# Moving the places at which the split weight buffers begin in SBUF

## The chip, the cores and the metric

The kernel runs on one core of one Trainium2 chip. Its time is the device time of one execution in microseconds (us).

## What is computed

Two transformer-like blocks over 256 tokens of width 2048, one after the other, all in float32. Cut to the products with large weights, which are nearly all of the work:

```python
# first block
h = rmsnorm(x, g[0]);  proj = h @ w_in                     # 2048 -> 6736
y_pool, y_conv, y_attn = mixers(proj)                      # small work beside
up    = einsum('bsnc,ncd->bsnd', [y_pool, y_conv, y_attn], w_branch)
gates = sigmoid(h @ w_gate + b_gate)                       # 2048 -> 3 * 2048
x = x + rmsnorm((sum(gates * up)) @ w_out, g[1])
x = x + rmsnorm(square(relu(rmsnorm(x, g[2]) @ w_up)) @ w_down, g[3])   # 2048 -> 8192 -> 2048
# second block
h = modulate(rmsnorm(x), silu(c) @ w_ada + b_ada);  p = h @ w_in_2
y = (g_a * ((attn * silu(z_a)) @ w_pa) + g_b * ((fourier(u_b) * silu(z_b)) @ w_pb)) @ w_o
out = rmsnorm(x + gate * y)
```

## The kernel before, in words

Every large product is a job, and every job is cut into chunks of KC = 2 blocks of 128 weight rows by 512 weight columns (512 KB, 4 KB in each partition). There are 768 chunks, numbered q, and each engine takes them in that order. A chunk passes through four hands:

1. SyncE loads it from HBM into one of five `raw` buffers.
2. ScalarE copies it into a high buffer `whi` in the format float32r (`high`, line 906).
3. VectorE subtracts the high part from the raw one and writes the rest into a low buffer `wlo` (`low`, line 1234). It works AHEAD = 3 chunks ahead of TensorE.
4. TensorE multiplies (`chunk`). The other operand, the activations, is split in the same way, into pairs such as `op0h` and `op0l`. Each product is three matmuls: high by high, high by low, low by high.

High and low buffers number NSPL = 4 each, and chunk q uses number q % 4. ScalarE may write a high buffer again when TensorE has finished the chunk four back.

A job has one of two modes. In mode T (280 chunks) the activations are the stationary operand, 128 columns, and the split weights are the moving one, 512 columns: 12 matmuls a chunk, lines 867, 868 and 869. In mode W (488 chunks) it is the other way round: the weights are stationary, 128 columns, and the activations move, 256 columns: 24 matmuls a chunk (18 in one job with 384 weight columns), lines 874, 875 and 876. Every matmul loads stationary weights of its own. One job, `vw`, is a mode T job with 272 moving columns in place of 512. Long runs of jobs in one mode follow each other; the order is that of `job_list`. Between chunks stand short side parts (transposes, attention scores, sums over partitions), for which TensorE leaves the chain of chunks for a moment.

Addresses in a partition: `line(shift)` moves the next free place to `shift` bytes past a multiple of 256. All operand buffers (`op0h`, `op1h`, `yah`, `hch`, `mgh` and their low halves) begin 64 bytes past a multiple of 256. In a split buffer, mode T chunks begin at 64 past it and mode W chunks at 128 past it. Inside a buffer the pieces that one matmul reads are 512, 1024 or 2048 bytes apart, so the place past a multiple of 256 is the same for all of them.

Of the kernel before, what the change touches and what calls it, by code (L numbers as in the profile page):

```python
# [10 lines left out]
ACT = mybir.ActivationFunctionType  # L11
AX = mybir.AxisListType.X
F32 = mybir.dt.float32
F32R = mybir.dt.float32r
# [3 lines left out]
KC = 2  # L18
NRAW = 5
NSPL = 4  # L20
# [118 lines left out]
def program(nc, a, out, scratch_e, scratch_x):  # L139
    ctx = ExitStack()  # L140
    with ctx:
# [51 lines left out]
        for u in range(12):  # L193
            q = of["vw"].end + 1 + 2 * u
# [6 lines left out]
        for g in range(4):  # L201
            q = (of["pool0"].end + 1, of["pool0"].end + 5, of["pool1"].end + 1, of["pool1"].end + 5)[g]
# [5 lines left out]
        for i in range(4):  # L208
            q = of["pool1"].end + 11 + 2 * i
# [5 lines left out]
        for i in range(4):  # L215
            q = of["q1"].end + 2 + 10 * i
# [10 lines left out]
        for j in range(12):  # L227
            q = ada_at[8 * j + 7]
# [3 lines left out]
        for tt in range(2):  # L232
            q = of["b23"].end + tt
# [3 lines left out]
            q = of["wo3"].end + 1 + tt  # L237
# [3 lines left out]
            q = of["dn33"].end + 1 + tt  # L241
            side(dve_at, q, "mlp_add", tt)
            q = of["dn33"].end + 2 + tt
# [3 lines left out]
        for s, q0 in ((1, of["wo0"].first + 6), (2, of["kc"].first + 5), (3, of["vc"].first + 7)):  # L247
            for i in range(8):
                q = q0 + i // 2
# [3 lines left out]
        for s, name in enumerate(("kc", "k", "qq0", "qq1", "qq2")):  # L253
            q = of[name].end
# [7 lines left out]
        for i in range(6):  # L262
            q = heads2[i]
# [10 lines left out]
        for g in range(4):  # L274
            q = of["zb"].end + 4 * g
# [8 lines left out]
        top = [(nc.sbuf_base + 63) // 64 * 64]  # L284

        def at(name, shape, off, dt=F32):
            return nc.alloc_sbuf_tensor_at(name, shape, dt, offset=off)

        def sb(name, shape, dt=F32):
            size = 4 * int(np.prod(shape[1:]))  # L290
            t = at(name, shape, top[0], dt)
            top[0] += (size + 31) // 32 * 32
            return t

        raw = [sb(f"raw{i}", [128, KC, 512]) for i in range(NRAW)]
        def line(shift):

            top[0] += (shift - top[0]) % 256
            return top[0]

        def split_buffers(name):

            w = {"T": [], "W": []}
            for i in range(NSPL):
                o = line(64)
                for mode, shift in (("T", 0), ("W", 64)):
                    w[mode].append(at(f"{name}{mode}{i}", [128, KC, 512], o + shift, F32R))
                top[0] = o + 64 + 4 * KC * 512
            return w

        whi, wlo = split_buffers("whi"), split_buffers("wlo")
        op0_at = line(64)
        op0h, op0l = sb("op0h", [128, 16, 256], F32R), sb("op0l", [128, 16, 256], F32R)
# [88 lines left out]
        def pair_of(job):  # L402
            return bank[2 * job.pair], bank[2 * job.pair + 1]
# [6 lines left out]
        def sem(name):  # L410
            return ctx.enter_context(nc.semaphore("s_" + name))

        s_raw = [sem(f"raw{i}") for i in range(NRAW)]
        s_hi, s_lo, s_pe = sem("chunk_high"), sem("chunk_low"), sem("chunk_done")
# [105 lines left out]
        landed, fills = {}, [0] * NRAW  # L520
# [91 lines left out]
        def _(pe):  # L612
# [217 lines left out]
            def operand_wait(job, k):  # L830

                if job.x in ("x0", "ctx", "x1", "x2"):
                    pe.wait_ge(s_oper, 8 * ("x0", "ctx", "x1", "x2").index(job.x) + k // 2 + 1)
                elif job.x == "pool":
                    pe.wait_ge(s_plo, k // 2 + 1)
                elif job.x == "conv":
                    pe.wait_ge(s_clo, k // 2 + 1)
                elif job.x == "ya":
                    pe.wait_ge(s_ya, k + 2)
                elif job.x == "mix":  # L840
                    pe.wait_ge(s_mix, k // 2 + 1)
                elif job.x == "att":
                    pe.wait_ge(s_att, k + 2)
                elif job.x == "four":
                    pe.wait_ge(s_four, k + 2)
                elif job.x == "mg":
                    pe.wait_ge(s_mg, k // 2 + 1)
                else:
                    pe.wait_ge(s_hid, 8 * job.arg[0] + k // 2 + 1)

            def chunk(q, tts=(0, 1)):
                job, k = chunks[q]
                banks = pair_of(job)
                xh, xl = hi_of[job.x], lo_of[job.x]
                h, l = whi[job.mode][q % NSPL], wlo[job.mode][q % NSPL]
                if k == 0 and job.before:
                    pe.wait_ge(s_pair[job.pair], job.before)
                if job.fresh:
                    operand_wait(job, k)
                pe.wait_ge(s_lo, q + 1)  # L860
                for kk in range(KC):
                    ka, first, last = job.kt0 + k + kk, k + kk == 0, k + kk == job.nkt - 1
                    if job.mode == "T":
                        for tt in tts:
                            o = banks[tt][:, 0:job.n]
                            th, tl = xh[:, ka, 128 * tt:128 * tt + 128], xl[:, ka, 128 * tt:128 * tt + 128]
                            pe.matmul(o, th, h[:, kk, 0:job.n], start=first, stop=False, skip_group_check=True)  # L867
                            pe.matmul(o, th, l[:, kk, 0:job.n], start=False, stop=False, skip_group_check=True)  # L868
                            mm = pe.matmul(o, tl, h[:, kk, 0:job.n], start=False, stop=last, skip_group_check=True)  # L869
                    else:  # L870
                        for m in range(job.n // 128):
                            o = banks[m // 2][:, 256 * (m % 2):256 * (m % 2) + 256]
                            wh, wl = h[:, kk, 128 * m:128 * m + 128], l[:, kk, 128 * m:128 * m + 128]
                            pe.matmul(o, wh, xh[:, ka, :], start=first and m % 2 == 0, stop=False, skip_group_check=True)  # L874
                            pe.matmul(o, wh, xl[:, ka, :], start=False, stop=False, skip_group_check=True)  # L875
                            mm = pe.matmul(o, wl, xh[:, ka, :], start=False, stop=last, skip_group_check=True)  # L876
                if 1 in tts:
                    mm.then_inc(s_pe, 1)
                elif q == NQ - 1:
                    mm.then_inc(s_o2first, 1)  # L880
# [7 lines left out]
            for q in range(NQ - NSPL):  # L888
                for name, arg in pe_at[q]:
                    parts[name](*arg)  # L890
                chunk(q)
            for tt in range(2):
                for q in range(NQ - NSPL, NQ):
                    chunk(q, (tt,))
# [4 lines left out]
        def _(act):  # L899
            def high(q):  # L900
                job, k = chunks[q]
                i, v = landed["w", q]
                act.wait_ge(s_raw[i], v)
                if q >= NSPL:
                    act.wait_ge(s_pe, q - NSPL + 1)
                act.activation(whi[job.mode][q % NSPL][:, :, 0:job.n], raw[i][:, :, 0:job.n], ACT.Copy).then_inc(s_hi, 1)  # L906

            def square(src, junk, name, tt):
                act.activation(junk, src[:, tt, :], ACT.Square, accum_out=norm_col(name, tt)[0]).then_inc(s_sumsq, 1)
# [301 lines left out]
            for i in range(3):  # L1211
                turn_x(i)
                high(i)
            for q in range(NQ):
                for name, arg in act_at[q]:
                    parts[name](*arg)
                if q + AHEAD < NQ:
                    high(q + AHEAD)
                if q in ends and ends[q].ep in eps:
                    if q < NQ - 1:  # L1220
                        act.wait_ge(s_pe, q + 1)
                    eps[ends[q].ep](ends[q], *pair_of(ends[q]))
# [4 lines left out]
        def _(v):  # L1227
            own = Steps(s_dve)

            def low(q):  # L1230
                job = chunks[q][0]
                x, h = raw[landed["w", q][0]][:, :, 0:job.n], whi[job.mode][q % NSPL][:, :, 0:job.n]
                v.wait_ge(s_hi, q + 1)
                v.tensor_tensor(wlo[job.mode][q % NSPL][:, :, 0:job.n], x, h.bitcast(F32), ALU.subtract).then_inc(s_lo, 1)  # L1234

            summed = [0, 0]

# [449 lines left out]
            for i in range(4):  # L1687
                x = x0[:, 1, 512 * i:512 * i + 512]
# [4 lines left out]
            for i in range(3):  # L1693
                turn_x(i)
                low(i)
            for q in range(NQ):
                for name, arg in dve_at[q]:
                    parts[name](*arg)
                if q + AHEAD < NQ:
                    low(q + AHEAD)  # L1700
                    for i in ada_after[q + AHEAD]:
                        ada(i)
                if q == NQ - 1:
                    ep_o2_last(ends[q], *pair_of(ends[q]))
                elif q in ends and ends[q].ep in eps:
                    v.wait_ge(s_pe, q + 1)
                    eps[ends[q].ep](ends[q], *pair_of(ends[q]))
# [24 lines left out]
```

## Time and profile before

| | us |
|---|---|
| median of 2 runs | 2303.47 (2302.29 to 2304.64) |
| the profiled execution | 2306.96 |
| its span, first to last instruction | 2305.1 |
| TensorE busy (matmuls) | 2274.0 (99%) |
| VectorE busy | 1468.4 (64%) |
| ScalarE busy | 1070.8 (46%) |
| mean granted TensorE clock | 0.996 of 2.4 GHz |

Matmuls are pipelined and their recorded durations overlap, so what counts for TensorE is not the duration of one but the step from the start of one to the start of the next. A window of the trace that holds nothing but matmuls gives it: its length by their number (two or three of those counted lie across its edges). The execution has 1.9 us outside its span.

### The profile page before, as it was taken

How to read it: one execution, taken by the hardware profiler on the slowest of the kernel's cores; microseconds unless marked ns; L12 is line 12 of the kernel's file. 1: busy time of each engine (PE TensorE's matmuls, PEld its weight loads, DVE VectorE, ACT ScalarE, POOL GpSimd, SP SyncE). 2: the span in 40 equal slices, each digit the busy share in tenths (PEclk: the TensorE clock that was granted, in tenths of full speed). 3: DMA queues.
4: the chain of work that ended last, by engine and by line, in shares of the span. 5: the costliest groups of instructions: out<-in, count | busy, mean ns of one | idle time of the engine just before them, and what ended most of it. 6: DMA issues, size and time to landing. Idle time of an engine off the chain costs nothing.

```text
span 2305.1 us, 37604 instructions
## 1 busy us (share of the span) xinstructions
PE 2274.0 (99%) x15980; PEld 2116.1 (92%) x15980; DVE 1468.4 (64%) x1844; ACT 1070.8 (46%) x1422; POOL 40.4 (2%) x61
## 2 busy tenths in 40 slices
PE   7999999999999999999999999999999999999998
PEld 7889999999999988988988988998889979999987
DVE  6757578787887667544555555555756545577665
ACT  5444435444344456544443443444656545434443
POOL 1000000000000001000000000000100000000000
PEclk9999999999999999999999999999999999999999
DMA  8855676677777765666656656656664444778763
GB/s 273 253 158 163 192 218 222 219 229 240 247 230 251 250 226 176 186 202 192 186 192 192 186 189 197 195 181 209 230 203 132 145 118 139 248 273 274 252 214 138
DMA packets 246368, 473.73 MB, mean 206 GB/s; under 512 B 21166, under 2 KB 25624, under 8 KB 244536
## 3 DMA queue, kind: packets, MB, share of 16 engines
q1 hardware_dynamic: 242888, 454.40, 61.8%
q0 software_dynamic: 3312, 16.92, 2.2%
q8 instruction: 126, 2.06, 0.4%
q14 instruction: 42, 0.34, 0.0%
HBM read 467.05 MB, written 4.21 MB: 204 GB/s over the span
## 4 chain that ended last, share of the span: by engine, by line
PE 95%; DVE 2%; DMA 1%; ACT 1%; issue 1%; POOL 0%; SPq 0%; POOLq 0%; ACTq 0%; DVEq 0%
PE ps L874 19%; PE ps L876 19%; PE ps L875 19%; PE ps L867 10%; PE ps L868 10%; PE ps L869 10%; PE ps L802 1%; PE ps L741 1%; PE ps L663 1%; DMA raw<-in_w_out 1%; PE ps L781 0%; PE ps L791 0%; PE ps L782 0%; DVE tmp L1260 0%; PE ps L637 0%
## 5 line engine op out<-in xcount | busy, mean ns | idle before, releaser
L874 PE MATMUL ps<-op0h,whiW 128*128 128x256 f32 x3248 | 918.5, 283 | 1.1 <-DVE wloW L1234 1.1
L875 PE MATMUL ps<-op0l,whiW 128*128 128x256 f32 x3248 | 910.4, 280 | 0.0
L876 PE MATMUL ps<-op0h,wloW 128*128 128x256 f32 x3248 | 910.3, 280 | 0.0
L1234 DVE TENSOR_TENSOR wloW<-raw,whiW 128x1024 fp32r<-128x1024 f32 (+1 forms) x488 | 591.3, 1219 | 415.5 <-ACT whiW L906 414.0
L906 ACT ACTIVATE whiW<-raw 128x1024 fp32r<-128x1024 f32 (+1 forms) x488 | 512.1, 1056 | 607.5 <-PE ps L876 533.5
L875 PEld LDWEIGHTS ps<-op0l,whiW 128*128 128x128 f32 x3248 | 616.9, 190 | 2.0 <-issue 1.4
L874 PEld LDWEIGHTS ps<-op0h,whiW 128*128 128x128 f32 x3248 | 612.6, 189 | 6.4 <-issue 5.8
L876 PEld LDWEIGHTS ps<-op0h,wloW 128*128 128x128 f32 x3248 | 615.1, 189 | 0.0
L1234 DVE TENSOR_TENSOR wloT<-raw,whiT 128x1024 fp32r<-128x1024 f32 (+1 forms) x280 | 336.2, 1210 | 288.8 <-ACT whiT L906 288.3
L906 ACT ACTIVATE whiT<-raw 128x1024 fp32r<-128x1024 f32 (+1 forms) x280 | 290.8, 1047 | 322.9 <-PE ps L869 269.2
L867 PE MATMUL ps<-whiT,op1h 128*128 128x512 f32 x640 | 249.6, 390 | 0.1
L868 PE MATMUL ps<-wloT,op1h 128*128 128x512 f32 x640 | 249.2, 389 | 0.0
L869 PE MATMUL ps<-whiT,op1l 128*128 128x512 f32 x640 | 249.1, 389 | 0.0
L1260 DVE SCALAR_TENSOR_TENSOR tmp<-raw,csil,tmp 128x512 f32<-128x512 f32 x300 | 209.4, 747 | 2.5 <-DMA raw<-in_w_ada 1.3
L867 PEld LDWEIGHTS ps<-whiT,op1h 128*128 128x128 f32 x640 | 120.2, 188 | 25.1 <-DVE wloT L1234 0.5
L869 PEld LDWEIGHTS ps<-whiT,op1l 128*128 128x128 f32 x640 | 120.2, 188 | 25.0
L874 PE MATMUL ps<-op1h,whiW 128*128 128x256 f32 x512 | 143.1, 279 | 0.0
L868 PEld LDWEIGHTS ps<-wloT,op1h 128*128 128x128 f32 x640 | 120.2, 188 | 24.5
L876 PE MATMUL ps<-op1h,wloW 128*128 128x256 f32 x512 | 142.5, 278 | 0.0
L875 PE MATMUL ps<-op1l,whiW 128*128 128x256 f32 x512 | 142.5, 278 | 0.0
L867 PE MATMUL ps<-whiT,op0h 128*128 128x512 f32 (+1 forms) x288 | 114.4, 397 | 0.0
L868 PE MATMUL ps<-wloT,op0h 128*128 128x512 f32 (+1 forms) x288 | 110.1, 382 | 0.0
(264 smaller groups left out, 2114.5 us busy)
## 6 DMA issues: line engine op xcount, KB each, us to landing
raw<-in_w_in SPq DMA_DIRECT2D x256, 512.0 KB, 4.3
raw<-in_w_up SPq DMA_DIRECT2D x128, 512.0 KB, 3.7
raw<-in_w_down SPq DMA_DIRECT2D x128, 512.0 KB, 3.8
raw<-in_w_ada SPq DMA_DIRECT2D x96, 512.0 KB, 4.6
raw<-in_w_gate SPq DMA_DIRECT2D x96, 512.0 KB, 4.6
raw<-in_w_out SPq DMA_DIRECT2D x64, 512.0 KB, 4.4
raw<-in_w_branch SPq DMA_DIRECT2D x48, 512.0 KB, 5.3
raw<-in_w_proj_a SPq DMA_DIRECT2D x24, 512.0 KB, 4.6
```

Of the source, the lines that this page charges most:

```text
L663: mm = pe.matmul(ps[:, j * nk:(j + 1) * nk], qb[lo:lo + 64, h // 2, 128 * tt:128 * tt + 128], kid[lo:lo + 64, 0:nk], start=True, stop=True)
L741: mm = pe.matmul(ps[:, 2 * m + f:2 * m + f + 1], tmp[f][:, 128 * m:128 * m + 128], ones[:, 0:1], start=True, stop=True)
L802: mm = pe.matmul(ps[:, 128 * tt:128 * tt + 128], vv[:, st % 2, 128 * kv:128 * kv + 128], p[:, 128 * st:128 * st + 128], start=st == 0, sto ...
L867: pe.matmul(o, th, h[:, kk, 0:job.n], start=first, stop=False, skip_group_check=True)
L868: pe.matmul(o, th, l[:, kk, 0:job.n], start=False, stop=False, skip_group_check=True)
L869: mm = pe.matmul(o, tl, h[:, kk, 0:job.n], start=False, stop=last, skip_group_check=True)
L874: pe.matmul(o, wh, xh[:, ka, :], start=first and m % 2 == 0, stop=False, skip_group_check=True)
L875: pe.matmul(o, wh, xl[:, ka, :], start=False, stop=False, skip_group_check=True)
L876: mm = pe.matmul(o, wl, xh[:, ka, :], start=False, stop=last, skip_group_check=True)
L906: act.activation(whi[job.mode][q % NSPL][:, :, 0:job.n], raw[i][:, :, 0:job.n], ACT.Copy).then_inc(s_hi, 1)
L1234: v.tensor_tensor(wlo[job.mode][q % NSPL][:, :, 0:job.n], x, h.bitcast(F32), ALU.subtract).then_inc(s_lo, 1)
L1260: op = v.scalar_tensor_tensor(o, w, c, o, ALU.mult, ALU.add)
```

## The change

A high and a low buffer no longer begin at a place that depends on the mode. Each buffer has four places, 0, 64, 128 and 192 bytes past a multiple of 256. The high part of chunk q uses place q // 2 % 4, the low part place q // 8 % 4, in both modes. The buffers are as far apart as before (4352 bytes), the numbers q % 4 stay, and so do all waits, instructions, sizes and their order. The operand buffers after them begin where they began.

```diff
@@ -300,12 +300,11 @@
         def split_buffers(name):
 
-            w = {"T": [], "W": []}
+            w = []
             for i in range(NSPL):
-                o = line(64)
-                for mode, shift in (("T", 0), ("W", 64)):
-                    w[mode].append(at(f"{name}{mode}{i}", [128, KC, 512], o + shift, F32R))
-                top[0] = o + 64 + 4 * KC * 512
+                o = line(0)
+                w.append([at(f"{name}{i}_{s}", [128, KC, 512], o + s, F32R) for s in range(0, 256, 64)])
+                top[0] = o + range(0, 256, 64)[-1] + 4 * KC * 512
             return w
@@ -852,7 +851,7 @@
-                h, l = whi[job.mode][q % NSPL], wlo[job.mode][q % NSPL]
+                h, l = whi[q % NSPL][q // 2 % 4], wlo[q % NSPL][q // 8 % 4]
@@ -903,7 +902,7 @@
-                act.activation(whi[job.mode][q % NSPL][:, :, 0:job.n], raw[i][:, :, 0:job.n], ACT.Copy).then_inc(s_hi, 1)
+                act.activation(whi[q % NSPL][q // 2 % 4][:, :, 0:job.n], raw[i][:, :, 0:job.n], ACT.Copy).then_inc(s_hi, 1)
@@ -1229,9 +1228,9 @@
-                x, h = raw[landed["w", q][0]][:, :, 0:job.n], whi[job.mode][q % NSPL][:, :, 0:job.n]
+                x, h = raw[landed["w", q][0]][:, :, 0:job.n], whi[q % NSPL][q // 2 % 4][:, :, 0:job.n]
                 v.wait_ge(s_hi, q + 1)
-                v.tensor_tensor(wlo[job.mode][q % NSPL][:, :, 0:job.n], x, h.bitcast(F32), ALU.subtract).then_inc(s_lo, 1)
+                v.tensor_tensor(wlo[q % NSPL][q // 8 % 4][:, :, 0:job.n], x, h.bitcast(F32), ALU.subtract).then_inc(s_lo, 1)
```

## Rows read from the trace of the kernel before

**Rows 1.** The page: TensorE's busy time and granted clock
```profile
PE 2274.0 (99%) x15980; PEld 2116.1 (92%) x15980; DVE 1468.4 (64%) x1844; ACT 1070.8 (46%) x1422; POOL 40.4 (2%) x61
...
PEclk9999999999999999999999999999999999999999
```

**Rows 2.** The page: chain of work that ended last, by engine
```profile
PE 95%; DVE 2%; DMA 1%; ACT 1%; issue 1%; POOL 0%; SPq 0%; POOLq 0%; ACTq 0%; DVEq 0%
```

**Rows 3.** Waits of TensorE: engine, line, waited for, total us, times, longest
```profile
PE ps L637 <- DVE x L1689: 11.7, 1, 11.7
PE ps L815 <- DVE op1l L1465: 4.8, 1, 4.8
...
PE ps L874 <- DVE wloW L1234: 1.1, 1, 1.1
PE ps L867 <- DVE wloT L1234: 0.9, 1, 0.9
```

**Rows 4.** Groups by shape, the split: count, busy us, mean ns, idle before
```profile
L1234 DVE TENSOR_TENSOR wloW<-raw,whiW 128x1024 fp32r<-128x1024 f32 x480 | 583.8, 1224 | 412.2 <-ACT whiW L906 410.7
L906 ACT ACTIVATE whiW<-raw 128x1024 fp32r<-128x1024 f32 x480 | 505.3, 1060 | 596.8 <-PE ps L876 524.9 <-PE ps L869 40.3 <-DMA raw<-in_w_in 18.5
L1234 DVE TENSOR_TENSOR wloT<-raw,whiT 128x1024 fp32r<-128x1024 f32 x272 | 330.5, 1224 | 287.0 <-ACT whiT L906 286.5
L906 ACT ACTIVATE whiT<-raw 128x1024 fp32r<-128x1024 f32 x272 | 285.5, 1058 | 316.0 <-PE ps L869 269.2 <-PE ps L876 37.8 <-DMA raw<-in_w_in 4.5
```

**Rows 5.** Groups by shape: the first of the three matmuls, modes W and T
```profile
L874 PE MATMUL ps<-op0h,whiW 128*128 128x256 f32 x3248 | 918.5, 283 | 1.1 <-DVE wloW L1234 1.1
...
L867 PE MATMUL ps<-whiT,op1h 128*128 128x512 f32 x640 | 249.6, 390 | 0.1
...
L874 PE MATMUL ps<-op1h,whiW 128*128 128x256 f32 x512 | 143.1, 279 | 0.0
```

**Rows 6.** Windows, TensorE alone: window, length, busy (count), clock, DMA share, GB/s
```profile
222.00:328.00 106.00, 106.00 (x897) 1.00 0.66 196
...
559.00:620.00 61.00, 61.00 (x520) 1.00 0.73 235
906.00:994.00 88.00, 88.00 (x779) 1.00 0.62 192
1082.00:1168.00 86.00, 86.00 (x733) 1.00 0.62 188
```

**Rows 7.** Windows, all engines, in mode T: busy (count) of PE, PEld, DVE, ACT, POOL
```profile
1180.00:1250.00 70.00, 70.00 (x311) 57.97 (x310) 34.97 (x32) 27.59 (x26) 0.00 (x0) 1.00 0.61 198
...
1360.00:1430.00 70.00, 70.00 (x311) 57.97 (x310) 34.73 (x33) 27.59 (x26) 0.00 (x0) 1.00 0.59 194
```

**Rows 8.** Timeline around two entries into mode W: start us, us
```profile
905.35 1.04 PE L637 MATMUL ps<-ident,macc 128*128 128x128 f32 x8
906.14 0.37 PE L874 MATMUL ps<-op0h,whiW 128*128 128x256 f32 x1
...
1081.04 0.39 PE L869 MATMUL ps<-whiT,op1l 128*128 128x512 f32 x1
1081.27 0.28 PE L874 MATMUL ps<-op0h,whiW 128*128 128x256 f32 x1
```

**Rows 9.** Timeline of a mode T chunk after transposes: its second and last matmul
```profile
809.51 0.39 PE L868 MATMUL ps<-wloT,op1h 128*128 128x512 f32 x1
...
811.82 0.39 PE L869 MATMUL ps<-whiT,op1l 128*128 128x512 f32 x1
```

**Rows 10.** Timeline of `vw`: fifteen matmuls, the first and the last
```profile
84.22 0.29 PE L867 MATMUL ps<-whiT,op0h 128*128 128x272 f32 x1
...
85.98 0.29 PE L869 MATMUL ps<-whiT,op0l 128*128 128x272 f32 x1
```

**Rows 11.** Timeline of attention scores, matmuls that read no split buffer
```profile
1723.39 0.59 PE L781 MATMUL ps<-ktx,qt 128*128 128x256 f32 x2
...
1726.41 0.59 PE L782 MATMUL ps<-ktc,qt 128*128 128x256 f32 x2
```

## The prediction

> **What bounds the kernel now.** I read five views, in this order. The page first: TensorE is busy for 2274.0 of 2305.1 us at full granted clock [rows 1], and the chain of work that ended last is 95% TensorE [rows 2]. So the time is the number of matmuls times their step, plus little. The waits of TensorE second: the largest is the start (11.7 us, the first normed rows), and a split buffer was waited for just twice, 1.1 and 0.9 us [rows 3]. The groups by shape third, for the split: the high copy takes 1060 ns in mode W and 1058 in mode T, the low subtraction 1224 in both, while a chunk lasts some 2.8 us of TensorE; both spend hundreds of us idle, ScalarE mostly until TensorE frees a buffer [rows 4]. The matmul groups show next to no idle time, but their durations (283, 279, 390 ns) overlap and can't be summed [rows 5].
>
> What can be summed is the step, from the windows, fourth. In mode W it has two values. From 1082 to 1168 us 733 matmuls are counted; less some two across the edges that is 86 / 731 = 117.6 ns. From 906 to 994 us it is 88 / 777 = 113.3 ns with the same instructions, the same shapes and addresses that are equal past a multiple of 256 [rows 6]. From matmul to matmul the timeline says 117.8 and 113.3. In mode T it is 70 / 309 = 226.5 ns, the same in both stretches [rows 7]; 226.7 from matmul to matmul. The DMA share is 0.62 in both the fast and the slow W stretch, and 0.66 and 0.73 in two slow ones, so traffic doesn't set it [rows 6]. A stretch keeps its value through dozens of chunks until TensorE does something else. The slow stretch at 1081 begins right behind a mode T matmul, 0.23 us from start to start; the fast one at 906 behind eight transposes, 0.79 us after their first [rows 8]. Going through the timeline chunk by chunk I count 330 of the 488 W chunks at 117.8, 156 at 113.3 and 2 that side parts break up.
>
> I read this as an interference between two streams that TensorE itself reads at once, the moving operand and the next stationary one: which of two self-repeating patterns it falls into depends on when it starts. Nothing here shows that mechanism; the rows show that timing alone moves a step by 4.4 ns. The fifth view is of chunks that haven't settled. After transposes a T chunk takes (811.82 - 809.51) / 10 = 231.0 ns a step [rows 9], against 226.7. `vw`, whose 272 columns don't fill a whole number of 256 byte blocks, never settles: (85.98 - 84.22) / 14 = 125.7 ns a step [rows 10]. At the rate per column of the settled patterns (113.3 / 256 = 226.7 / 512 = 0.443 ns) it would be 120.4, so disorder costs it 5.3 ns, 4%.
>
> **The change part by part.** It moves where the high and low buffers begin and nothing else. Against the operands, which stay at 64 past a multiple of 256, T chunks always had place 64 and W chunks place 128. Now a chunk has its old high place in one of four cases, its old low place in one of four, both in one of sixteen. The high place changes every second chunk, so a job of eight chunks goes through all four.
>
> Writing the buffers (ScalarE, VectorE): the mode T and mode W buffers lie 64 bytes apart and take 1058 against 1060 ns and 1224 against 1224 [rows 4]. 768 chunks times 2 ns would be 1.5 us on an engine that idles. I take nothing; the cover is 2.8 us of TensorE per chunk against 1.06 and 1.22, and without it 768 x 1.22 = 937 us of subtraction would still be less than the matmuls. Loads, waits, queues: unchanged in number and order, nothing. Waits on the buffers stay by q % 4, and views at different places of one buffer share it, as T and W views did: nothing.
>
> Reading them (TensorE): every step is on the path. There are 480 x 24 + 8 x 18 = 11664 W steps and 280 x 12 = 3360 T steps. At present the W steps take about 330 x 24 x 117.8 + 156 x 24 x 113.3 ns = 1357 us and the T steps 3360 x 226.7 ns = 762 us, together 2119 of 2305; the rest is side parts and the start. No row shows another place, so the price has two sides. Down: fast W everywhere would give 330 x 24 x 4.45 ns = 35 us; still lower would need steps such as those of the transposes, (1.04 - 0.28) / 7 = 109 ns [rows 8], and of the scores, (1726.41 - 1723.39) / 14 = 215.7 ns [rows 11], which read no split buffer: 11664 x 7.4 + 3360 x 11 ns = 123 us. Up: the 5.3 ns of `vw` on every step is 80 us; on T in proportion to its columns (4%, 10 ns) the sum is 62 + 34 = 96 us.
>
> I choose in between. In mode W a pattern that holds for dozens of chunks needs a relation of places that repeats. With a new one every second chunk I expect the fast stretches to be lost, and W at the slow 117.8 throughout, which is nearest to the rows since 330 of 486 chunks have it already: 156 x 24 x 4.45 = 17 us. In mode T I expect half of the steps unsettled at 231.0: 1680 x 4.3 ns = 7 us. The sum is 24 us: 2307.0 + 24 = 2331 for an execution like the one profiled. That one is 3.5 above the median of the runs shown, so 2303.5 + 24 = 2327.
>
> The Trainium skill speaks against any effect. The page "SBUF — State Buffer", section "Who interferes with whom", says that TensorE has separate read ports for the moving operand and for weight loads, and that it and ScalarE never wait on anyone; its cachelines are 16 bytes, which steps of 64 leave alone. By that rule nothing changes and the result is 2303. The two W steps in rows 6 show that something in TensorE's reads does depend on timing, so I don't take it as the likeliest. The page "TensorE: Matmul & The Clock Gate", section "Back-to-back issue gap", gives N / 2.4 + 2.5 ns, which is 109.2 and 215.8 ns for 256 and 512 columns; an estimate by it would be 2303 - 11664 x 7.2 - 3360 x 10.9 ns = 2183. The settled steps of this trace, 113.3 and 226.7, lie above it.
>
> **The rivals.**
>
> Places don't matter (2303, within 8): the two patterns are a matter of when streams start, and 64 bytes don't enter. For it: DMA and engines change beside a stretch without a trace in its step, and all seven long entries from T into W without a break fall in the same slow pattern. Against: if streams meet by address, a shift in place is a shift in time.
>
> The changing place frees the slow stretches (2269 to 2295): W settles at 113.3 in all or most chunks, up to -35 us, with T as it is. For it: 330 chunks have this to gain, and a fast stretch often follows a disturbance. Against: as many disturbances end in the slow pattern.
>
> Some places are bad (2375, slower by 3%). One mechanism: in some relations of high or low place to the operand at 64, the reads of both streams meet on every pass, in each step of the chunk, not just in unsettled ones. The nearest price is that of `vw` and of the first steps of T chunks after a break, which I put at 5 to 10 ns a step; 15024 steps at a mean of 4.8 ns are 72 us. It decides from a mean of 3.1 ns a step (46 us, 2%), that is when about half of the relations cost over 6 ns. For it: T sits at its settled step in place 64 in every long stretch, and leaving it can only be level or a loss as far as any split row shows. Against: no row has such a relation.
>
> All steps fall to those of matmuls that read no split buffer (2183). Against it: no split matmul comes near in any stretch.
>
> It does what it says: the places are constants of the program. What it may miss is independence: buffers 0 and 1 take only the high places 0 and 128, buffers 2 and 3 only 64 and 192. All four come equally often, so the sums stand.
>
> **How the numbers follow.** Forecast (24 us, 2327): 0.33. Places don't matter: 0.22. Bad places: 0.30. Slow stretches freed: 0.12. All steps fall: 0.03. About 2% (46 us) is what a measurement of this kernel can tell from no change. Faster by over 2%: the last case and the extreme of the freed one, 0.04. Slower by over 2%: 0.27 of the bad places and 0.04 of the forecast, 0.31. Within: 0.65. The range leaves out the last case, half of the freed one and the top third of the bad places, 0.19: 2285 to 2390.
>
> **What would show each step.** The groups of the split should keep 1060 and 1224 ns, and TensorE's waits for `wlo` stay below 5 us. The windows 1180 to 1250 and 1082 to 1168 should no longer have one step each: in T I expect two kinds of chunks, near 226.7 and near 231; in W 117 to 119. If a step follows the place (the same for every chunk with one combination), the places act by themselves and the bad-place rival is right in kind; if it follows breaks alone, the first rival is. I am wrong if T falls below 226, if W is at 113 for most chunks, or if the split comes onto the chain.

## The result and the profile after

| | before | after |
|---|---|---|
| median, us | 2303.47 | 2330.39 (2329.87 to 2330.92, 2 runs) |
| profiled execution, us | 2306.96 | 2329.87 |
| its span, us | 2305.1 | 2328.0 |

The change makes the kernel slower by 1.2%: ratio 1.0116, 95% interval 1.0091 to 1.0140. The forecast was 2327.

The page of the changed kernel, its engines and the chain by engine, answers to [rows 1, 2]:

```profile
PE 2297.8 (99%) x15980; PEld 2127.3 (91%) x15980; DVE 1468.1 (63%) x1844; ACT 1071.0 (46%) x1422; POOL 40.4 (2%) x61
...
PEclk9999999999999999999999999999999999999999
...
PE 97%; DVE 1%; issue 1%; DMA 1%; ACT 0%; SPq 0%; POOL 0%; POOLq 0%; DVEq 0%; ACTq 0%
```

TensorE is busy 23.8 us longer for the same 15980 matmuls at the same granted clock. The other engines did the same work in the same time. Their groups by shape, with modes T and W now under one name, answer to [rows 4], and the first and the last row to [rows 5]:

```profile
L873 PE MATMUL ps<-op0h,whi 128*128 128x256 f32 x3248 | 919.0, 283 | 1.3 <-DVE wlo L1233 1.3
L1233 DVE TENSOR_TENSOR wlo<-raw,whi 128x1024 fp32r<-128x1024 f32 x752 | 914.0, 1223 | 720.7 <-ACT whi L905 719.6
...
L905 ACT ACTIVATE whi<-raw 128x1024 fp32r<-128x1024 f32 x752 | 791.1, 1059 | 935.0 <-PE ps L875 580.9 <-PE ps L868 319.4 <-DMA raw<-in_w_in 20.3
...
L866 PE MATMUL ps<-whi,op1h 128*128 128x512 f32 x640 | 252.2, 394 | 0.0
```

The copy takes 1059 ns and the subtraction 1223 at four places instead of two. TensorE's waits are the old ones too, from its view of waits (before: [rows 3]):

```profile
PE ps L636 <- DVE x L1688: 11.8, 1, 11.8
...
PE ps L873 <- DVE wlo L1233: 1.3, 1, 1.3
...
PE ps L866 <- DVE wlo L1233: 0.7, 1, 0.7
```

So the loss is in the steps. Added up over the chunks, start to start, mode W takes 12.9 us more, mode T 9.6, and the start and the last four chunks 0.4: together 22.9, the difference of the spans. That is 4.0 less than the 26.9 between the medians, since the profiled execution of before lies 3.5 above its median and that of after 0.5 below.

Part of that excess is visible, and it hides in the 9.6. The whole T chunks of 512 columns take 11.9 us more after the change, and the job `vw` 2.3 us less. In the profiled execution of before TensorE idled for 1.64 us ahead of the side part in that job, and the granted clock behind it was 0.50 (1.2 GHz) from 96 to 98 us; after the change it idled for 0.74 us there and kept 1.00. The windows behind it, before and then after:

```profile
96.00:98.00 2.00, 2.00 (x10) 0.50 0.99 348
...
96.00:100.00 4.00, 4.00 (x20) 1.00 0.90 296
```

**The step follows the pair of places.** The timeline of the changed kernel, first and last matmul of four whole chunks. First W at high 64, low 64 (24 matmuls), then W at 128 and 0 (24), T at 0 and 64 (12), T at 64 and 64 (12):

```profile
914.78 0.28 PE L873 MATMUL ps<-op0h,whi 128*128 128x256 f32 x1
...
917.54 0.28 PE L875 MATMUL ps<-op0h,wlo 128*128 128x256 f32 x1
...
988.97 0.28 PE L873 MATMUL ps<-op0h,whi 128*128 128x256 f32 x1
...
991.58 0.28 PE L875 MATMUL ps<-op0h,wlo 128*128 128x256 f32 x1
...
1000.24 0.40 PE L866 MATMUL ps<-whi,op1h 128*128 128x512 f32 x1
...
1002.83 0.39 PE L868 MATMUL ps<-whi,op1l 128*128 128x512 f32 x1
...
1005.82 0.39 PE L866 MATMUL ps<-whi,op1h 128*128 128x512 f32 x1
...
1008.31 0.39 PE L868 MATMUL ps<-whi,op1l 128*128 128x512 f32 x1
```

That is 2.76 / 23 = 120.0, 2.61 / 23 = 113.5, 2.59 / 11 = 235 and 2.49 / 11 = 226 ns a step. All whole chunks of 512 columns read in this way (the mean step of a chunk's second half, then the median over the 12 to 32 chunks of a pair) give a table for each mode, in ns, with the high place down and the low place across:

```
mode T      0     64    128    192      mode W      0     64    128    192
   0    233.3  234.3  231.3  231.1         0    117.8  117.8  113.3  115.6
  64    228.8  226.7  231.8  229.0        64    117.8  120.0  117.8  118.8
 128    231.2  233.3  233.3  232.2       128    113.3  117.8  117.8  118.2
 192    231.2  228.9  232.2  232.5       192    120.0  118.3  117.8  118.8
```

In mode T the old pair (64, 64) is the fastest of the sixteen. In mode W the old pair (128, 128) is middling, and (128, 0) ran at 113.3 in all of its 28 chunks; (0, 128) did so in 20 of 28. Several entries are medians of chunks that differ: of the 18 T chunks at (128, 128) twelve ran at 233.3 and six at 228.8 to 229.0. Means over all chunks of 512 columns without breaks: T 227.0 before and 231.3 after, W 116.4 and 117.7.

### The profile page after: what moved, and what is told of

Read it like the earlier page. It is cut to its first block, busy times and chain, and to the rows that moved or that the text cites. A ratio compares the mean times of both kernels' runs of the same rounds, so it can differ in the third digit from the quotient of the medians.

```text
span 2328.0 us, 37604 instructions
## 1 busy us (share of the span) xinstructions
PE 2297.8 (99%) x15980; PEld 2127.3 (91%) x15980; DVE 1468.1 (63%) x1844; ACT 1071.0 (46%) x1422; POOL 40.4 (2%) x61
## 4 chain that ended last, share of the span: by engine, by line
PE 97%; DVE 1%; issue 1%; DMA 1%; ACT 0%; SPq 0%; POOL 0%; POOLq 0%; DVEq 0%; ACTq 0%
PE ps L873 20%; PE ps L874 20%; PE ps L875 19%; PE ps L866 11%; PE ps L867 11%; PE ps L868 11%; PE ps L801 1%; PE ps L740 1%; PE ps L636 1%; PE ps L662 1%; PE ps L780 0%; PE ps L781 0%; PE ps L790 0%; PE ps L814 0%; PE ps L686 0%
## 5 line engine op out<-in xcount | busy, mean ns | idle before, releaser
L1233 DVE TENSOR_TENSOR wlo<-raw,whi 128x1024 fp32r<-128x1024 f32 (+1 forms) x768 | 927.2, 1215 | 727.0 <-ACT whi L905 725.9
L905 ACT ACTIVATE whi<-raw 128x1024 fp32r<-128x1024 f32 (+1 forms) x768 | 803.1, 1053 | 952.9 <-PE ps L875 593.3
L873 PE MATMUL ps<-op0h,whi 128*128 128x256 f32 x3248 | 919.0, 283 | 1.3 <-DVE wlo L1233 1.3
L874 PE MATMUL ps<-op0l,whi 128*128 128x256 f32 x3248 | 910.6, 280 | 0.0
L875 PE MATMUL ps<-op0h,wlo 128*128 128x256 f32 x3248 | 910.3, 280 | 0.0
L873 PEld LDWEIGHTS ps<-op0h,whi 128*128 128x128 f32 x3248 | 612.2, 188 | 6.5 <-issue 5.9
L874 PEld LDWEIGHTS ps<-op0l,whi 128*128 128x128 f32 x3248 | 612.1, 188 | 2.0 <-issue 1.4
L875 PEld LDWEIGHTS ps<-op0h,wlo 128*128 128x128 f32 x3248 | 613.1, 189 | 0.0
L866 PE MATMUL ps<-whi,op1h 128*128 128x512 f32 x640 | 252.2, 394 | 0.0
L867 PE MATMUL ps<-wlo,op1h 128*128 128x512 f32 x640 | 252.1, 394 | 0.0
```

Source lines behind the costliest of these rows:

```text
L905: act.activation(whi[q % NSPL][q // 2 % 4][:, :, 0:job.n], raw[i][:, :, 0:job.n], ACT.Copy).then_inc(s_hi, 1)
L1233: v.tensor_tensor(wlo[q % NSPL][q // 8 % 4][:, :, 0:job.n], x, h.bitcast(F32), ALU.subtract).then_inc(s_lo, 1)
```

## The experiments

Two theories stand against each other. P: each pair of places has its own step, whatever came before. L, my forecast's mechanism: patterns are settled into, breaks and changes of place end them, and the places act only by changing. Each edit is against the changed kernel; `[..]` stands for the index of the place, 0 to 3 for 0 to 192 bytes, at all uses of the high and the low buffer. The kernel before was run again beside each group of experiments (medians 2302.3, 2302.9 and 2303.5 us), and each ratio is to those runs. Of each kernel one execution was traced, so counts of chunks are those of one execution.

**e1_best_pair**: T at 64 and 64, W at 128 and 0.

```diff
-whi[q % NSPL][q // 2 % 4]                      wlo[q % NSPL][q // 8 % 4]
+whi[q % NSPL][1 if job.mode == "T" else 2]     wlo[q % NSPL][1 if job.mode == "T" else 0]
```

> T chunks stay at places 64 and 64 as before; all W chunks take high place 128 and low place 0, the pair at which the changed kernel's chunks ran at 113.3 ns a step in 28 of 28 cases. Theory P, each pair of places has a step of its own: all W steps become 113.3, the 330 chunks that ran at 117.8 give 330 x 24 x 4.45 ns = 35 us, result near 2268 us. Theory L, the step is set by breaks and by the places' changing, not by the places: W shows the two patterns of the kernel before, result 2303 us, within 8.

Measured: 2271.08 us (4 runs), ratio to before 0.9861 (0.9846 to 0.9875). P holds. Windows of TensorE in this kernel (window, length, busy and count, clock, DMA share, GB/s), three in mode W and the last in mode T, against [rows 6, 7]:

```profile
240.00:320.00 80.00, 80.00 (x709) 1.00 0.69 208
550.00:602.00 52.00, 52.00 (x461) 1.00 0.77 250
886.00:970.00 84.00, 84.00 (x743) 1.00 0.63 193
975.00:1055.00 80.00, 80.00 (x355) 1.00 0.59 192
```

With two matmuls across the edges these are 113.2, 113.3, 113.4 and 226.6 ns. The stretches around 240 and 550, slow before the change, are now as fast as any. Between the two profiled executions the W chunks take 35.3 us less than before the change, as P has it; between the medians it is 31.2.

**e2_only_t and e3_only_w**: one mode takes the changing places, the other its old pair.

```diff
 e2: high [q // 2 % 4 if job.mode == "T" else 2]   low [q // 8 % 4 if job.mode == "T" else 2]
 e3: high [1 if job.mode == "T" else q // 2 % 4]   low [1 if job.mode == "T" else q // 8 % 4]
```

> Only T chunks take the changing places; W chunks have 128 and 128 as before the change. Both theories: T goes from 227.0 to 231.3 ns a step, 3360 x 4.3 ns = 14.5 us; W stays at 116.4. Near 2318 us. My prediction's own term for T was 7 us, which would be 2310.

> Only W chunks take the changing places; T chunks have 64 and 64 as before the change. W goes from 116.4 to 117.7 ns a step, 11664 x 1.27 ns = 15 us, T stays at 226.7. Near 2318 us. If the two halves of the change don't add up (e2 and e3 together unlike 27 us), modes hand something over at their borders.

Measured: e2 2312.65 us, ratio 1.0040 (1.0026 to 1.0055); e3 2317.14 us, ratio 1.0060 (1.0045 to 1.0075). The increases are 10.4 and 14.9 us, together 25.3 of the 26.9. In e2 T steps are 231.4 ns as expected, which is 14.6 us by the steps and 13.1 added up over the whole T chunks of 512 columns. But W steps fell from 116.4 to 116.0 (5 us): the pair (128, 128) has two patterns, and 285 chunks were in the slow one instead of 330. I read this as T chunks at another pace handing over to W at other moments; no run shows it by itself, and another execution might differ as well. It is small.

**e4_w_at_operand**: every chunk at 64 and 64, never changing.

```diff
 high [1]   low [1]
```

> All chunks, T and W, have places 64 and 64, never changing: the operands' own place. Theory P: W steps are 120.0 ns everywhere, as in 32 of 32 chunks with that pair, 11664 x 3.6 ns = 42 us slower than before, near 2345 us, slower than the changed kernel although nothing changes from chunk to chunk. Theory L: nothing changes from chunk to chunk, so the two patterns of the kernel before come back, 2303 us.

Measured: 2344.37 us, ratio 1.0178 (1.0161 to 1.0195). P holds, to a microsecond. Two windows in mode W and one in mode T of e4:

```profile
250.00:335.00 85.00, 85.00 (x711) 1.00 0.65 195
922.00:1010.00 88.00, 88.00 (x736) 1.00 0.60 185
1015.00:1095.00 80.00, 80.00 (x355) 1.00 0.59 193
```

W is at 85 / 709 = 119.9 and 88 / 734 = 119.9 ns, T at 226.6; all W chunks but one that a side part breaks up are at 119.9 or 120.0. A kernel in which no place ever changes is slower than the one that goes through all of them, so the changing isn't the cost.

**e5_t_bad_pair**: as e1, T at 0 and 64.

```diff
-high [1 if job.mode == "T" else 2]
+high [0 if job.mode == "T" else 2]
```

> As e1 (W at high 128, low 0, 2271 us), but all T chunks have high place 0 and low place 64, never changing: the pair at which the changed kernel's T chunks ran slowest, 234.3 ns a step. Theory P: 3360 x 7.3 ns = 25 us more than e1, near 2296 us, with T at 234.3 throughout. Theory L for mode T, the loss comes from the places' changing between chunks: T settles at 226.7 or near it and the result is 2271 us.

Measured: 2294.13 us (5 runs, 2292.9 to 2298.5), ratio to before 0.9968 (0.9955 to 0.9981), 23.1 us more than e1. Mode T in a window of e5, which stands against the last row of e1:

```profile
985.00:1065.00 80.00, 80.00 (x343) 1.00 0.58 191
```

80 / 341 = 234.6 ns; the T chunks of 512 columns are at 234.0 to 234.7 in this kernel but for one at 247.3, so P holds for T too.

**e6_all_moved**: as e1, with the operands and all weight places 64 bytes further on.

```diff
-op0_at = line(64)      op1_at = line(64)      big = line(64)
+op0_at = line(128)     op1_at = line(128)     big = line(128)
 high [2 if job.mode == "T" else 3]   low [2 if job.mode == "T" else 1]
```

> As e1 with everything moved by 64 bytes: operands at 128 instead of 64, T chunks at 128 and 128, W chunks at high 192 and low 64. Theory P-relative, only the places of the weights relative to the operands count: same as e1, 2271 us. Theory P-absolute, the place past a multiple of 256 counts by itself: T as the pair 128 and 128 (231.9, 16 us more), W as the pair 192 and 64 (118.3, 58 us more), near 2345 us.

Measured: 2270.13 us, ratio 0.9857 (0.9841 to 0.9874), that of e1 (0.9861). W at 113.3 in all 488 chunks, T at 226.7. What counts is where high and low weights lie relative to the operand, not any address by itself. (The 231.9 of the expectation is the mean of the pair (128, 128), the 233.3 of the table its median.)

**e7_finer**: the changed kernel with eight places 32 bytes apart.

```diff
-range(0, 256, 64)    high [q // 2 % 4]   low [q // 8 % 4]
+range(0, 256, 32)    high [q // 2 % 8]   low [q // 16 % 8]
```

> The changed kernel with eight places 32 bytes apart: high place q // 2 % 8, low place q // 16 % 8. One look at the step of each of 64 pairs. If 64 bytes is the grain of the interference, places 32 bytes off give steps like one of their neighbours and the time stays near 2330 us. If it is finer, they have values of their own, perhaps below 113.3 (W) or 226.7 (T), which no pair has gone below so far.

Measured, in a single run: 2337.91 us. Each pair has just 2 to 10 chunks here. Places 32 bytes off have steps of their own: T at high 96, low 64 takes 233.3 ns between 227.9 and 231.2 at high 64 and 128; W at high 128, low 32 takes 117.2 between 113.3 and 117.8 at low 0 and 64. So 64 bytes isn't the grain. No pair went below 226.7 or 113.3. W at high 192 and low 0, 120.0 in the changed kernel, was 115.6 here, and W at 128 and 128 was 113.3 where it had been 117.8: some pairs have more than one pattern, and what comes before them chooses.

**e8_low_operand**: the changed kernel with `op0l` and `op1l` 64 bytes further on than `op0h` and `op1h`.

```diff
-op0h, op0l = sb("op0h", ...), sb("op0l", ...)
+op0h = sb("op0h", ...)
+line(128)
+op0l = sb("op0l", ...)        # op1h, op1l likewise
```

> The changed kernel with the low halves op0l and op1l moved to 128 while op0h and op1h stay at 64 (other operands as before). One look at the 16 pairs again. Theory P-relative: each of the three matmuls of a group has another relation to its neighbours, so the table of pairs changes; the mean should stay near that of the changed kernel, 2330 us within 15. If a pair goes below 113.3 or 226.7, those aren't the floor.

Measured, in a single run: 2342.03 us. The chunks that read the moved halves have another table: T is 231.1 at (64, 64) and 228.8 at best, W 113.3 in no pair and 117.1 at best. The chunks of the same run whose operands weren't moved (`yah`, `hch`, `mgh`) keep 226.7 at (64, 64) in four chunks and 113.3 at (128, 0) in the two that there are. That is P-relative again, within one run. It also says that it isn't the addresses to which ScalarE and VectorE write the split weights: these are the same as in the changed kernel, and the table is another.

**e9_two_good_pairs and e10_other_good**: W changes every second chunk between (0, 128) and (128, 0); W stays at (0, 128). T at 64 and 64 in both.

```diff
 e9:  high [1 if job.mode == "T" else q // 2 % 2 * 2]   low [1 if job.mode == "T" else 2 - q // 2 % 2 * 2]
 e10: high [1 if job.mode == "T" else 0]                low [1 if job.mode == "T" else 2]
```

> T at 64 and 64. W chunks change every second chunk between two pairs (high, low) that both gave 113.3 ns: 0 and 128, then 128 and 0. Theory P: changing costs nothing by itself, W stays at 113.3 except where a break puts the pair 0 and 128 into its second pattern (118.9 ns in the changed kernel), and the next change of place ends that; near 2271 us as e1, at most 10 more. Theory L, as in my prediction: a relation that changes every second chunk can't hold a fast pattern, W goes to 117.8, 11664 x 4.5 ns = 52 us more than e1, near 2323 us.

> T at 64 and 64, all W chunks at high place 0 and low place 128, never changing. In the changed kernel this pair had two patterns, 113.3 in 20 chunks and 118.9 in 8, all 8 behind a break. Theory P with two patterns: fast where nothing breaks the chain, slow in stretches that a break put there and nothing ends, so slower than e1 (2271 us) and e9: between 2280 and 2310 us. If it gives 2271, the pair is as good as 128 and 0, and the slow chunks came from the changing.

Measured: e9 2276.30 us, ratio 0.9879 (0.9865 to 0.9894); e10 2300.09 us, ratio 0.9986 (0.9976 to 0.9995). e9 settles the point on which my forecast rested: with a change every second chunk W holds 113.3 in 451 chunks and is at 118.8 or 118.9 in just 36, all of them at (0, 128). e10 never changes and loses 29 us against e1: 249 of its W chunks are at 113.3 and 238 at 118.8 to 119.0, and 238 x 24 x 5.5 ns = 31 us. Every slow stretch of the two kernels begins right behind a break. Two windows of mode W in e10, one in each pattern:

```profile
245.00:325.00 80.00, 80.00 (x708) 1.00 0.66 204
560.00:615.00 55.00, 55.00 (x465) 1.00 0.75 240
```

That is 113.3 and 118.8 ns, with the same pair. So P in its strict form, a step of the pair's own whatever came before, is false too; by it e10 would have been at 2271. A pair has one or more settled patterns: (128, 0) one in all runs, (0, 128) and (128, 128) two each. Where there are two, a break or an entry picks one, and it stays until the next break or change of place. In e9 the changes end the slow pattern; in e10 nothing does.

## Why the prediction was right, and where its mechanism wasn't

**Bound and cover: right.** TensorE's steps are the time. The split costs nothing at any place (1059 and 1223 ns), and its waits stayed at 1.3 and 0.7 us against the 5 that I allowed.

**The size: right, in part by luck.** 24 us were forecast and 26.9 measured between the medians. The parts are known from the profiled executions, 22.9 us apart: W 17 forecast and 12.9 found, T 7 forecast and 9.6 found (11.9 without `vw`). So one term was too large, the other too small, and the errors partly cancelled.

**The step that failed in mode W** is "a pattern that holds for dozens of chunks needs a relation of places that repeats. With a new one every second chunk I expect the fast stretches to be lost, and W at the slow 117.8 throughout". In its place: each pair brings its own step. The mean of 117.7 comes from pairs at 113.3 and at 120.0, and no chunk needs a run-up of dozens; e9 changes every second chunk and costs 5 us against e1, e4 never changes and costs 73. I got near the sum since 117.8 happens to be close to the mean over the pairs, which is luck. The sign that I gave for the windows, W at 117 to 119, failed as well: single chunks lie at 113.3 to 120.0.

**The step that was too small in mode T** is "half of the steps unsettled at 231.0". The chunks aren't unsettled: fifteen of the sixteen pairs have steps of 228.8 to 234.3, so nearly all lose, 231.3 in the mean, and there are many values where I expected two kinds. e5 shows it with one pair that never changes. That leaving (64, 64) could be only level or a loss was right.

**A price that was misread.** The prediction takes 109 ns of the transposes and 215.7 ns of the scores for what the split steps of 113.3 and 226.7 could fall to, in its 123 us and in its last rival. But the rows give these matmuls 128 and 256 moving columns, half of those of the split ones that they stand beside [rows 8, 11]. Per column they take 109 / 128 = 0.85 and 215.7 / 256 = 0.84 ns against 0.443. They are another kind of matmul, plain float32 in the program where the split ones are float32r, and no row of this case gives a price below 113.3 and 226.7. The sum of the forecast doesn't use them.

**The rivals.** "Places don't matter" is refuted by e4 and e5. Of what it rested on, the entries from T into W without a break are six in the trace, not seven, all slow; the three entries behind a break are all fast, at the same places. The Trainium skill's page "SBUF — State Buffer", section "Who interferes with whom", with independent read ports for TensorE's two operands and a TensorE that waits on no one, would give that result; the measured 2271 to 2344 us for places alone say that the rule leaves something out, and the measurement decides. (The cachelines of 16 bytes that the prediction adds stand in the Trainium skill's page "Advanced Engine Details and Errata", section "SBUF Cachelines"; no run here shows them.) "Some places are bad" was right in kind and named its sign beforehand: one relation, in each step of the chunk. Its price was too high: the worst pairs cost 7.6 ns in T and, against the old mean, 3.6 in W, not a mean of 4.8 over all, so it stayed within 2%. "The changing place frees the slow stretches" was false for this change but true of one with good pairs: e9 is 27 us faster than before, and e1 31.

**What stays open.** The runs show that the relation between the operands' places and the weights' decides, that moving everything together changes nothing, and that moving low operands alone does. That it is the moving read meeting the next stationary read within TensorE fits this, and is argued, not shown: no kernel took one of the two reads away. Why (128, 0) has a single pattern is open too, and so is what in a break picks one of two. e7 and e8 are single runs; what rests on them alone (that 32 bytes matter, and that low operands moved by themselves change the table) has one trace each.

## What to carry to other kernels

When TensorE is busy for 99% of the span, read its step from start to start, by stretch: two values for the same matmul are time to be had, here 31 us between the medians. A kernel that walks buffers through combinations of places is a poor kernel but a good probe. One run gave a table of sixteen pairs for each mode, and two lines of it (T at 64 and 64, W at high 128 and low 0 with the operands at 64) made the fastest version here, 2271 us (2270 with everything moved by 64 bytes), 1.4% under the kernel before and 2.5% under the changed one. Prefer a pair with one pattern to one that is sometimes as fast.

## What the runs showed of the hardware that I had not expected

- The start of a matmul's weights relative to its other operand, down to shifts of 32 bytes, moves the step: 113.3 to 121.1 ns (7%, the 121.1 in e7 and e8) for 256 moving float32r columns with new stationary weights each time, 226.7 to 234.5 (3.4%) for 512.
- No stretch of split matmuls in any run went below 113.3 and 226.7 ns; both are 0.443 ns a column. From the Trainium skill's page "TensorE: Matmul & The Clock Gate", section "Back-to-back issue gap", 109.2 and 215.8 ns are estimates; its formula is for an isolated matmul, and for a stream at 512 columns it has about 131 ns. The measured 226.7 lies above both, and that section names no type of data.
- The same pair of places can run in two settled patterns, 113.3 and 118.9 ns at (0, 128), and keep one over several chunks until something breaks it.
